# Dense product of a PEER decoder step: u columns in 128 transfers of 1 MB through two buffers

## The reference, cut to what matters

```
act = gelu(einsum('thkd,td->thk', peer_u[idx], hb))
return einsum('thk,thkd->td', w * act, peer_v[idx])
```

## Time and profile before

| what | value |
|---|---|
| median of three executions | 5396.97 us |
| the profiled execution | 5362.92 us |
| its span | 5361.1 us |
| TensorE busy, share of the span | 75% |
| VectorE | 52% |
| GpSimd | 25% |
| ScalarE | 7% |
| DMA, mean over the span | 264 GB/s |
| the dense product, first to last matmul | 3468.7 to 4413.4 us |

### The profile page before, as it was taken

One profiled execution on the slowest core, in us unless ns is written; L12 is line 12 of the kernel. 1 busy time (PEld: TensorE's weight loads), 2 busy tenths in 40 slices (PEclk: granted clock), 3 DMA queues, 4 the chain that ended last, 5 costly groups with the idle time before them and its releaser, 6 DMA issues.

```text
span 5361.1 us, 38323 instructions
## 1 busy us (share of the span) xinstructions
PE 4029.9 (75%) x14110; PEld 2429.6 (45%) x14110; DVE 2772.7 (52%) x3563; ACT 391.5 (7%) x822; POOL 1366.4 (25%) x1241
## 2 busy tenths in 40 slices
PE   7999688888779999999999796999999990000000
PEld 5887445554229984755555443544443430000000
DVE  1001732222110001587767666786765447799998
ACT  1000321222010000000000001000000000000000
POOL 0000000001430000124445443112222117777533
PEclk8999888778779999999999898999999995555555
DMA  3221141101446664668999987499999989999999
GB/s 138 76 70 63 52 151 67 35 23 39 147 127 243 241 233 149 241 264 362 413 406 414 409 338 284 185 364 397 388 403 419 357 326 344 344 400 409 416 422 381
DMA packets 234186, 1413.00 MB, mean 264 GB/s; under 512 B 34704, under 2 KB 35536, under 8 KB 86416
## 3 DMA queue, kind: packets, MB, share of 16 engines
q0 software_dynamic: 138960, 916.70, 43.1%
q1 hardware_dynamic: 81984, 458.79, 22.9%
q10 hardware_dynamic: 13088, 35.50, 1.7%
HBM read 1385.08 MB, written 25.75 MB: 263 GB/s over the span
## 4 chain that ended last, share of the span: by engine, by line
PE 53%; DMA 19%; DVE 11%; issue 8%; POOL 7%; ACT 2%; ACTq 0%; DVEq 0%; POOLq 0%
PE psum L811 15%; PE psum L542 10%; DMA arena<-in_v,arena 10%; PE psum L939 9%; DMA arena<-in_u_cols 7%; POOL arena L504 3%; PE psum L920 3%; DVE psum L1775 3%; POOL arena L522 2%; PE psum L850 2%; POOL arena L472 1%; PE psum L873 1%; PE psum L730 1%; DVE arena L1653 1%; PE psum L714 1%
## 5 line engine op out<-in xcount | busy, mean ns | idle before, releaser
L811 PE MATMUL psum<-arena 128*128 128x160 f32 (+1 forms) x5120 | 1175.7, 393 | 4.1 <-DVE arena L1508 3.3
L1775 DVE SCALAR_TENSOR_TENSOR psum<-arena,psum 128x2048 f32<-128x2048 f32 x381 | 897.3, 2355 | 193.4 <-DMA arena<-in_v,arena 178.0
L811 PEld LDWEIGHTS psum<-arena 128*128 128x128 f32 x5120 | 835.6, 190 | 343.7 <-issue 4.1
L939 PE MATMUL psum<-arena 128*128 128x512 f32 x2048 | 915.2, 600 | 32.2 <-DMA arena<-in_u_cols 26.9
L504 POOL DMA_INDIRECT arena<-in_v,arena x544 | 611.6, 1124 | 926.7 <-DVE arena L1653 371.4
L504 POOL DMA_INDIRECT arena<-in_u,arena x288 | 380.9, 1323 | 1440.0 <-DVE arena L1596 629.8
L542 PE MATMUL psum<-arena 128*128 128x272 f32 x2432 | 579.8, 402 | 80.7 <-ACT arena L1027 44.3
L939 PEld LDWEIGHTS psum<-arena 128*128 128x128 f32 x2048 | 378.7, 190 | 568.1 <-issue 419.1
L542 PEld LDWEIGHTS psum<-arena 128*128 128x128 f32 x2432 | 472.0, 195 | 185.3 <-issue 75.6
L1752 DVE CUSTOM_DVE_ANT_0 arena<-arena,psum 128x2048 f32<-128x2048 f32 x128 | 290.5, 2286 | 146.7 <-DMA arena<-in_u,arena 146.4
L465 POOL COPY stage_idx<-pages 128x16 uint32 x8 | 1.5, 194 | 1423.3 <-PE psum L700 1290.8
(11 more groups left out here) (267 smaller groups left out, 2950.0 us busy)
## 6 DMA issues: line engine op xcount, KB each, us to landing
arena<-in_w_merge SPq DMA_DIRECT2D x160, 1024.0 KB, 5.1
arena<-in_u_cols SPq DMA_DIRECT2D x256, 512.0 KB, 10.2
arena<-in_w_out SPq DMA_DIRECT2D x32, 1024.0 KB, 4.9
arena<-in_w_query SPq DMA_DIRECT2D x32, 1024.0 KB, 4.8
arena<-in_w_proj SPq DMA_DIRECT2D x31, 1024.0 KB, 4.8
products<-arena ACTq DMA_DIRECT2D x32, 512.0 KB, 12.3
arena<-in_v,arena POOLq DMA_INDIRECT x544, 11.1
arena<-in_w_mem_k SPq DMA_DIRECT2D x8, 1024.0 KB, 4.8
```

The lines of the kernel that those rows point to most:

```text
L811: last = mm(out, w[:, (off + k) * P:(off + k + 1) * P], src[:, k0 + k, lo:hi], start=(k == 0), stop=(k == n - 1))
L939: last = mm(psum[:, 4 + DENSE * (b % 2) + t, :], hfT_b[:, k0 + k, t * P:(t + 1) * P], u_tiles[n % 4][:, k, :], start=(k0 + k == 0), stop=( ...
L1775: V.scalar_tensor_tensor(a, four(row), atmp_b[:, t, r:r + 1], a if r else four(x1_b[:, t, :]), ALU.mult, ALU.add).then_inc(s("rows_used"), 1)
```

## The change

A new view splits the same 16 KB per partition into two buffers of 8 KB in place of four of 4 KB. SP issues 128 transfers of two tiles each. Pair m may be issued when pair m-2 has been used whole. TensorE waits for the pair in which its tile lies; the matmuls and the places that they read are as before. The host lays the columns out so that a partition's 8 KB of one pair are contiguous.

```diff
         u_tiles = [region(RINGAT + n * 1024, 2, 512) for n in range(4)]
+        u_pairs = [region(RINGAT + n * 2048, 2, 2, 512) for n in range(2)]
...
-            for n in range(256):
-                eng.wait_ge(s("w_used"), WEIGHTS + max(0, n - 3))
-                eng.dma_start(u_tiles[n % 4], A["u_cols"][n]).then_inc(ring_landed[n % 4], 16)
+            for m in range(128):
+                eng.wait_ge(s("w_used"), WEIGHTS + max(0, 2 * m - 2))
+                eng.dma_start(u_pairs[m % 2], A["u_cols"][m]).then_inc(ring_landed[m % 2], 16)
...
             for n in range(256):
                 b, k0 = n // 8, 2 * (n % 8)
-                pe.wait_ge(ring_landed[n % 4], U_LANDED[n % 4] + 16 * (n // 4 + 1))
+                pe.wait_ge(ring_landed[n // 2 % 2], U_LANDED[n // 2 % 2] + 16 * (n // 4 + 1))
...
-    A["u_cols"] = np.ascontiguousarray(f["peer_u"].reshape(32, 512, 8, 2, P).transpose(0, 2, 4, 3, 1)).reshape(256, P, 2, 512)
+    A["u_cols"] = np.ascontiguousarray(f["peer_u"].reshape(32, 512, 4, 2, 2, P).transpose(0, 2, 5, 3, 4, 1)).reshape(128, P, 2, 2, 512)
```

## The result

Over four executions the changed kernel takes 5495.22 us (5487.49 to 5504.45), the kernel before, four times, 5395.02 (5388.49 to 5401.4). The ratio is **1.0185, 95% interval 1.0166 to 1.0204**, or +100 us. Forecast were +37 us and slower with 0.67; 5495 lies outside the range of 5372 to 5472.

The account below looks back on a forecast made before the run. The dense product was taken to bound the kernel, with VectorE and GpSimd waiting for it. Block 25 33 us later plus 3 to 4 us to block 31 made +37 us, 5434 us; the 8-in-10 range was 5372 to 5472.

Parts of the forecast that it names:

- What bounds the kernel: Dense product: VectorE waits for it after blocks 5 and 25, GpSimd before its first gather of products, 57.4 us.
- the round of one buffer: Product beside gathers: with two buffers a pair takes (L + 7.14 + 0.08)/2, where landing L is over 6.5 us.
- L in the first stretch: Landing of a 1 MB pair from 3526 to 3980 us: 8.2 us, so 30.8 us a block, before 28.9.
- block 5: VectorE's first wait for the product: block 5 ends at 3652 us, 11 us late.
- block 25: Product before VectorE's tanh: block 25 ends at 4268 us, 33 us after 4235.
- block 1: Start of the product: first pair lands 1.3 us later, block 1 ends at about 3529 us, 3 us later.
- VectorE through the u rows: VectorE's u rows: 11 us late, faster gathers give back 7 and 5 us, so they end at 4186.
- from there to block 31: Product after block 25: 182 us in place of 178.9, 3 to 4 us more.
- the clock: TensorE in the product: granted clock stays at 1.00, as gaps of some 1.2 us a pair don't suggest less.
- C: Product from block 1 on: pairs land in 9.2 us everywhere, 32.8 us a block, +65 us, 5462; chance 0.25.
- A: Full-engine stretch: product gets half share, L 7.3 us, -23 us, 5374; at most -57 if landing in 6.5; chance 0.23 for both.
- D: Pair loads: pairs don't go in 8 KB packets; at 4 KB, L about 11.7 us, loss over 117 us; chance 0.03.

Follow-up runs that it names:

- the kernel with three pairs: The changed kernel with a third pair buffer, in the 8 KB of the final gain, which is loaded after the last block: ratio 0.9879 to the kernel before, 5305.02 us.
- six tiles: The kernel before with six 512 KB buffers in place of four, in the same 24 KB per partition as three pair buffers, 4 KB packets: ratio 0.994 to before.
- the kernel with 4 KB packets: The changed kernel with each pair loaded as two 512 KB transfers in 4 KB packets, TensorE waiting for both: ratio 1.0302 to the kernel before, +165 us.

## Why the prediction was wrong

**What bounds the kernel** was right. The product is the chain, it holds up VectorE after blocks 5 and 25 and GpSimd after 31, all three waits grew, and what follows GpSimd's gather is the same work. The direction was right, and so was the round of one buffer, (L + 7.22)/2: with the 9.4 us of the chain it gives 33.2 us a block, and 33.5 were measured.

**The term that failed is L in the first stretch.** I took 8.2 us, the middle of 9.2 and of 9.2 scaled by 9.5/12.1, the landings of the tiles before in the two stretches. With zeros in the gaps, so at full clock, a block takes (4169.62 - 3535.95)/19 = 33.35 us up to block 20, a pair 8.34, L = 2 x 8.34 - 7.22 = 9.5. On the change's own chain it is 9.3 up to 4000 us and 9.4 after; in the kernel with three pairs the median is 9.3 from 3521 to 3980 and 9.5 after. It is the same in both stretches. The scaling had no basis. A tile's landing before was mostly its wait behind the other tiles of its own queue: with five in line instead of three it is 19.8 us. At 28.9/8 = 3.61 us a tile, a landing of 9.5 means 2.6 tiles under way; at 31.3/8 = 3.91, 12.1 means 3.1. That fewer in line, and not room in the engines, made it 9.5 is likely but wasn't tried by itself. A pair alone in its queue landed no earlier beside the sparser gathers of the first stretch (119.41 MB in 536 us, 223 GB/s) than beside the denser ones of the second (54.37 MB in 190 us, 286 GB/s). The row of weight loads, 9.2, was the right one, and nothing should have been put in the place of it. Why a pair takes 9.4 us and not the 7.3 of an even share stays open.

**Step by step**, in the first profile, from its own start (19.4 us taken off): block 1 at 3530.6 (forecast 3529); block 5 at 3661.2 (3652); VectorE through the u rows at 4202 (4186), as the faster gathers gave back 5 us rather than 12; block 25 at 4316.1 (4268); from there to block 31 189.1 us (182). With L = 9.5 in place of 8.2 the same sum has blocks of 33.4 us: with VectorE at 4202, 6 + 538/33.4 = 22.1 blocks are done, block 25 ends at 4309, the rest takes 184: **+79 us**. That leaves 12 us, 7 up to block 25 and 5 behind it. The second failed term, the clock, which I had set at nothing, is large enough for them: 22.8 us on the chain. That the 12 us are the clock's, and why they aren't more, is not shown. I had reasoned with an even gap of 1.2 us a pair. TensorE in fact often works through two pairs and then stands longer at once: from 3550 to 4221 us its matmuls waited 47 times for a pair, 90.5 us in all and up to 3.5 us at once, where the waits before were at most 1.0 us (40 of them from 3526 to 4207 us, 19.5 us in all).

**The rivals.** C, landing at 9.2 us everywhere, comes nearest to what came: +65 us forecast. I gave it 0.25 and less than my middle value; it had both of the longer rows on its side. A fell for two buffers: of the 36 loads on the chain one landed in under 7.3 us (7.05). But its mechanism is real, and with a third buffer it is what pays: the three pairs gain 35 us more than six tiles in the same memory. D didn't happen; the kernel with 4 KB packets shows what it would have cost, +165 us. The Trainium skill's rule of 1 MiB or more per transfer (DMA: Bandwidth & Descriptors, Rules for kernel authors) came out both ways here, slower by 1.85% with two buffers and faster by 1.2% with three. Of those 1.2% the 8 KB of memory more give half, as the six tiles show.

## What to carry to other kernels

Larger transfers in the same memory mean fewer buffers, and what counts is the time from the release of a buffer to the moment when its data is needed: here it shrank from three tiles' work (10.3 us) to one pair's (6.9), and beside the gathers 1 MB took 9.4. Take that landing from transfers of the same size and packets, alone in their queue, beside the same other traffic; the landing of a queue with several in line says how long the line is. Where queues share the engines packet by packet, as here, larger packets are worth having, once there is a third buffer for them.

## What the runs showed of the hardware that was not expected

The granted clock fell from 1.00 to 0.97, 0.94 and 0.90 in stretches in which TensorE still worked 82% to 87% of the time. These are means of stretches at 2.4 GHz and short ones at 1.2 GHz, 13, 24 and 13 of them in the product of the change's three profiles. The waits of the kernel before, up to 1.0 us each, left it at 1.00. With the change's waits, up to 3.5 us each, it fell: from 3606.6 to 3609.26 us TensorE stood still after 14 us of matmuls, and the pair that followed took 8.85 us in place of 7.15, with a granted clock of 0.50 from 3610 to 3612 us. Other waits of the same length left it as it was, and how often it fell changed from one execution to the next (0.97 and 0.94 in the same kernel). Matmuls on zeros in the gaps, with waits of up to 2.1 us left, brought it back to 1.00.
